# One vector addition moved ahead of the next item's weight splits in a fused transformer and RWKV step

## The reference, cut to what matters

```
def swiglu(h, w_gate, w_up, w_down):
    return (jax.nn.silu(h @ w_gate) * (h @ w_up)) @ w_down

h = rmsnorm(x, ffn_norm[i, 0])
x = x + 0.5 * swiglu(h, ffn_w_gate[i, 0], ffn_w_up[i, 0], ffn_w_down[i, 0])
```

## Time and profile before

| | us |
|---|---|
| median of 3 runs | 3133.12 (3126.78 to 3135.42) |
| the profiled execution | 3126.64 |
| its span, first to last instruction | 3124.8 |
| PE busy | 2981.5 (95%) |
| DVE busy | 2113.6 (68%) |
| ACT busy | 1358.1 (43%) |
| POOL busy | 720.5 (23%) |
| mean granted clock of TensorE | 0.981 |

### The profile page before, as it was taken

How to read it: one execution, slowest core, us unless ns; L and a number is a source line. 1 busy time by engine, 2 the same in 40 slices (tenths; PEclk the granted TensorE clock), 3 DMA queues, 4 the chain that set the end, 5 groups by cost and what they waited for, 6 DMA issues and landing times.

```text
span 3124.8 us, 69564 instructions
## 1 busy us (share of the span) xinstructions
PE 2981.5 (95%) x29051; PEld 2866.5 (92%) x29051; DVE 2113.6 (68%) x2677; ACT 1358.1 (43%) x2411; POOL 720.5 (23%) x557
## 2 busy tenths in 40 slices
PE   7999999999999989999999999999799997899999
PEld 7999997599999979999999999999788886899999
DVE  5977866656566654878868788754456655478976
ACT  4433434455555543344443443424444543334432
POOL 1322210410000002123311133330145443212321
PEclk9999999999999999999999999999899999899999
DMA  3232212111111102222222322212000001223222
GB/s 114 93 98 90 86 65 72 38 35 35 37 53 48 62 14 69 81 95 89 90 92 82 95 85 91 95 55 99 5 11 15 14 18 40 74 76 95 87 90 85
DMA packets 78975, 208.24 MB, mean 67 GB/s; under 512 B 25505, under 2 KB 42274, under 8 KB 63714
## 3 DMA queue, kind: packets, MB, share of 16 engines
q1 hardware_dynamic: 78690, 204.16, 20.3%
HBM read 198.63 MB, written 5.49 MB: 65 GB/s over the span
## 4 chain that ended last, share of the span: by engine, by line
PE 86%; DVE 7%; ACT 4%; issue 2%; POOL 1%; DMA 0%; POOLq 0%; SPq 0%; DVEq 0%; ACTq 0%
PE PS L440 24%; PE PS L285 22%; PE PS L1553 11%; PE PS L2378 7%; PE PS L2123 5%; PE PS L613 5%; PE PS L1534 1%; PE PS L1580 1%; PE PS L2103 1%; DVE DOWN L740 1%; DVE WL L269 1%; DVE WL L406 1%; DVE X L744 1%; PE PS L297 1%; PE PS L1178 1%
## 5 line engine op out<-in xcount | busy, mean ns | idle before, releaser
L379 POOL TENSOR_TENSOR WLF<-RAW 128x512 f32<-128x512 f32 x72 | 94.0, 1306 | 975.7 <-PE PS L285 655.2
L264 ACT ACTIVATE WH<-RAW 128x1536 fp32r<-128x1536 f32 (+3 forms) x113 | 173.2, 1533 | 323.7 <-PE PS L285 202.0
L269 DVE TENSOR_TENSOR WL<-RAW,WH 128x1536 fp32r<-128x1536 f32 (+3 forms) x112 | 218.4, 1950 | 127.4 <-ACT WH L264 127.4
L1553 PE MATMUL PS<-UKMH,CTH 128*128 128x384 f32 (+1 forms) x768 | 269.1, 350 | 0.8 <-POOL RQL L1497 0.8
L440 PE MATMUL PS<-XH,WH 128*128 128x288 f32 x864 | 254.7, 295 | 8.3 <-DVE M L481 8.3
L440 PE MATMUL PS<-XH,WL 128*128 128x288 f32 x864 | 255.0, 295 | 0.0
L440 PE MATMUL PS<-XL,WH 128*128 128x288 f32 x864 | 254.4, 294 | 0.0
L1627 DVE TENSOR_REDUCE SS<-SQ 128x4 f32<-128x512 f32 x256 | 173.5, 685 | 119.4 <-ACT SQ L1612 117.4
L1553 PE MATMUL PS<-UKMH,CTL 128*128 128x384 f32 (+1 forms) x768 | 252.4, 329 | 0.0
L285 PE MATMUL PS<-HH,WH 128*128 128x288 f32 x1056 | 225.9, 295 | 4.1 <-DVE WL L269 4.1
L1612 ACT ACTIVATE SQ<-PS 128x384 f32<-128x384 f32 (+1 forms) x384 | 172.3, 455 | 131.8 <-PE PS L1553 131.8
(11 more groups left out here) (610 smaller groups left out, 9052.6 us busy)
## 6 DMA issues: line engine op xcount, KB each, us to landing
RAW<-in_w SPq DMA_DIRECT2D x113, 1024.0 KB, 4.9
RAW<-in_w SPq DMA_DIRECT2D x48, 768.0 KB, 4.9
ROWS<-in_cache_c SPq DMA_DIRECT2D x128, 128.0 KB, 2.0
RAW<-in_w SPq DMA_DIRECT2D x16, 512.0 KB, 4.4
ROWS<-in_cache_kr SPq DMA_DIRECT2D x128, 32.0 KB, 1.8
RAW<-in_w SPq DMA_DIRECT2D x8, 384.0 KB, 3.2
X<-in_x SPq DMA_DIRECT2D x4, 576.0 KB, 7.9
out_y<-X SPq DMA_DIRECT2D x8, 288.0 KB, 2.3
```

The source lines that it names most:

```text
L264: act.activation(WH[n % 2][:, 0:cols], RAW[n % 2][:, 0:cols], ACT.Copy).then_inc(rounded, 1)
L269: dve.tensor_tensor(WL[n % 2][:, 0:cols], RAW[n % 2][:, 0:cols], WH[n % 2][:, 0:cols].bitcast(F32), ALU.subtract).then_inc(item_split, 1)
L1553: mm = pe.matmul(out[:, 0:c1 - c0], c[u][:, x], w, start=t == 0, stop=t == 5)
```

## The change

In the first block-product item of every part that has them (x == 0, 12 times in the program), the addition `rest_dve` is issued directly behind `first_sum_dve` of the next item. It stood behind the three low parts (`gate_own_dve` twice, `first_lo_dve`). For all other items the order is the same. Nothing is added or removed, and no semaphore or wait is altered.

```diff
         if more:
             first_sum_dve(dve, n + x + 1, js + x + 1)
+            if x == 0:
+                rest_dve(dve, n, js)
             gate_own_dve(dve, n + x + 1, js + x + 1)
             first_lo_dve(dve, n + x + 1, js + x + 1)
         else:
             split_item(dve, n + x + 1, cols=2 * cnt * P)
         if x:
             hidden_dve(dve, j + x - 1, n + x - 1, False)
-        rest_dve(dve, n + x, js + x)
+        if x:
+            rest_dve(dve, n + x, js + x)
```

## The result

| | us |
|---|---|
| before, median of 22 runs | 3130.47 (3126.03 to 3135.42) |
| changed, median of 22 runs | 3134.72 (3131.65 to 3139.07) |
| ratio, 95% interval | 1.0015 [1.0009, 1.0021] |
| span of the profiled execution | 3132.5 (3124.8 before) |

What follows compares the result with a forecast made beforehand. PE, busy 95% of the span, was taken as the bound, so only its waits matter. Each of four parts sums to -2.31 + 0.73 + 2.44 = +0.86, +3.4 in all; from median 3133.12 to 3136.5 us, range 3125 to 3142.

Steps and rivals of the forecast that it cites:

- The stall removed: First item of part 1, ahead of block 4: PE's wait for the addition goes wholly, -2.31 us a part.
- S1's low part: Ahead of part 1's second item: the moved addition delays this low part, a new stall of 0.65 + 0.08 = 0.73 us.
- POOL set off early: Part 1: POOL starts the third item's sums at 109.47 and meets DVE's three low parts.
- The upper bound: Loss of DVE's three low parts meeting POOL's sums: 3 x 1.1 = 3.3 us taken, from bounds of 0 to 3.3.
- The evacuation and the copy: Part 1's second item: late evacuation delays ACT's second copy, block 6 begins at 117.01, a new stall of 2.44 us.
- The part in sum: Each of four parts: -2.31 + 0.73 + 2.44 = +0.86 us.
- The eight other places: First items of parts 2 and 3: the addition waits some 0.35 us for block 7, PE sees none of it, 0.
- Rival 3, the clock: Half-clock stretches follow the longer stall in all four parts instead of one: +8.5 us, 3141.6; chance 0.10.

Runs made afterwards that it cites:

- e3: Changed kernel, with the second copy of part 1's second item in its own place, not waiting for the evacuation; two items 24.62 us, timed once.
- e4: Changed kernel, with POOL's sums for part 1's third item held until DVE's last low part of the second; 0.9977 against before, two items 23.53 us.
- e2: Kernel before, with the addition moved only in the first items of parts 2 and 3 (8 of 12 places); two items 24.53 us, timed once.
- e1: Kernel before, with the addition moved only in the first item of part 1 (4 of 12 places); two items 25.18 us, timed once.
- e8: Kernel of e6 with POOL's wait left out, so its sums are not held; two items 25.18 us, timed once.
- e5: Kernel before, addition not moved, POOL's sums for all but a part's first item held until DVE's last low part of the item before; 0.9973 against before.
- e6: Changed kernel, addition behind L370 in all items but a part's last, S1's low part between the own two, sums held from third item; 0.9965 against before.

## Why the prediction was right, point by point

The forecast was 3136.5 us, +3.4 by a stall that moves to the second item. The median is 3134.72, and the ratio gives +4.7 us with 2.8 to 6.6 as its interval; the trace gives +2.6 at full clock. The mechanism is right step by step. That +3.4 lies inside the interval of the times is partly luck: the sum of a part was 0.2 us too high, and the trace's own 2.6 lies just outside. Most of the distance between 3136.5 and 3134.72 is the starting point, the median of three runs of before, 3133.12, which 22 runs put at 3130.47.

- *The stall removed* (2.31 a part): right. L481 is 0.60 behind L370, block 4 starts 9.51 after the first matmul with no idle, in all four parts.
- *S1's low part* (a new stall of 0.65 and 0.08): right in kind, 0.54 measured and 0.1 of restart. The low part ended where it was forecast, 108.80 + 0.69 - 97.89 = 11.60 us after the start (11.61 forecast). Too high was the 0.15 taken from the addition for PE to go on: here PE started 0.05 after it.
- *POOL set off early*: right. It starts 109.31 - 97.89 = 11.42 us after the first item's start, and 109.47 - 98.05 = 11.42 was forecast. It meets all three low parts at the prices of the pattern that was taken for it (1.78 and 3.48). The upper bound was the right one to take: the rows it came from have the same instructions in the same order, with POOL ahead by 0.14 there and by 0.10 here.
- *The evacuation and the copy* (block 6 at 117.01, that is 18.96 after the start): right in mechanism, confirmed by e3 and e4, measured 116.64 - 97.89 = 18.75. The sum was 0.2 us a part too high here. Most of it is the step that let L489 start 0.06 after the last low part; it overlapped it, as the rows of DVE do, and started 16.63 after the start in place of 16.80.
- *The part in sum*: +0.65 in place of +0.86.
- *The eight other places*: right, e2.
- *Rival 3, the clock*: not borne out, and not ruled out. It had more of the long stalls followed by a stretch at half clock after the change. In the profile of before one of four was, after two of four. But part 1 runs in e2 as before, and there it was three of four, and in e1 as changed, and there it was one of four. Together that is 4 of 8 with the stall ahead of block 4 and 3 of 8 with the stall ahead of block 6 (5 of 12 with e8). The price is shown: the window of two items is 26.73 with such a stretch and 25.18 without, 1.55 us, where 1.7 was worked out from the earlier trace rows. Here is that stretch of the first feed-forward after:

```profile
116.70:120.10 3.40, 3.40 (x14) 3.40 (x15) 3.40 (x6) 1.75 (x3) 0.00 (x0) 0.50 0.63 265
```

So it stays open why the times give +4.7 us and the trace 2.6. The mean granted clock points to the clock, 0.9772 over the 22 runs of the changed kernel against 0.9779 over the 17 of before that were taken beside e1 to e4, which is some 0.0007 x 3130 = 2.2 us. But single runs of before lie anywhere from 0.976 to 0.980, and the profiles do not show the missing stretches behind the stalls of part 1. No run changed the clock alone.

The same holds for the surplus of e4 and e5, some 3 and 4 us. None of their eight stalls ahead of a last block, nor of the four of e3, was followed by a stretch at half clock. If half of the four stalls of before are, as in the two profiles above (4 of 8), that is 4 x 0.5 x 1.5 = 3 us, an estimate, which would about make up the difference. For e6, 4 x 2.27 = 9.1 us by the trace and 11.0 by the ratio need no explanation, since the interval of the ratio is 6.9 to 15.3.

The difference of 7.7 us between the two spans does not come from the change alone. Between the third feed-forward's start and the fourth's the changed kernel took 1101.94 us and the one before 1102.61; between the first's and the second's it took 7.2 us more, of which the first two items of part 1 make 2.2. In the remaining 5.0 the order differs only in the first items of parts 2 and 3, which take 11.11 us in both. The difference goes with the clock elsewhere. Without the first five block-product items that stretch took 1146.2 us before, with 27.3 us at half clock in it, and 1151.2 after, with 41.0. Over all ten profiles the two go together, from 1146.1 us with 27.3 (e2) to 1152.0 with 44.4 (e3), without regard to what was changed. For one piece of it, about the same in both, the windows are these (before, then after; the clock is the number ahead of the last two):

```profile
540.00:650.00 110.00, 98.80 (x438) 64.87 (x438) 69.70 (x175) 51.31 (x122) 39.34 (x45) 0.98 0.18 48
540.00:650.00 110.00, 99.67 (x414) 64.62 (x412) 65.80 (x169) 48.31 (x114) 39.28 (x45) 0.92 0.16 42
```

A difference between two single profiles' spans is thus no measure of a change of a few us; the same stretch at full clock is.

## What to carry to other kernels

A stall that another engine ends can be a price paid to a third engine some us earlier: before an instruction is moved ahead, look whether those in front of it are as short as they could be. An instruction released by the engine that is made faster starts earlier too; find what it will lie beside, and if it shares something with that, hold it back by one wait so that more of it lies beside work it does not disturb. With such a wait a reordering took the two items from 23.53 to 22.26 us; without it neither of the two reorderings tried got below 25.18, where the kernel before had 24.53.

## What the runs showed of the hardware

- A vector instruction with both inputs in SBUF and a POOL instruction on 512 columns hold each other up. Where both queues were full they took turns, one pair in 1.70 us, and each of DVE's 512-column instructions took 1.78 us in place of 0.68 (changed, e3, e8), 1.10 more. POOL's took 1.62 in place of 1.30 from the second on. Where only a part of the time was shared the price was less: 2.17 in place of 1.82 for the two of L406 in e2. An addition that reads PSUM took 0.44 to 0.46 beside POOL as without it, and POOL's sum beside the additions stayed at 1.30 (e4).
- In the block products, 9 of 20 stalls of 2.2 to 2.8 us were followed by a stretch of 3.4 us at half clock (before, changed, e1, e2 and e8: 1, 2, 1, 3, 2 of 4 each), and none of 12 stalls of 0.6 to 1.7 us (e3, e4 and e5). Each such stretch cost about 1.5 us, as much as two thirds of the stall itself. It is a count of what happened to occur, not a test, and the length of one stall does not decide it: in the profile of before, among small matmuls of the second layer, TensorE was idle for 0.98 us and the clock fell 1 us later.

```profile
2395.48 0.33 PE L2438 MATMUL PS<-STC,GM 64*64 64x64 f32 x4 [0.98 <-ACT GAM L2692]
...
2396.50:2399.90 3.40, 3.40 (x72) 3.40 (x69) 1.84 (x2) 0.92 (x3) 3.19 (x3) 0.51 0.02 5
```
